# Query and key chunks of the even mixer as k-halves of 512 columns, rotations by token tile

## What is computed

```python
def rotate_pairs(t, cos, sin):
    t1 = t[..., 0::2]
    t2 = t[..., 1::2]
    return jnp.stack([t1 * cos - t2 * sin, t1 * sin + t2 * cos], axis=-1).reshape(t.shape)

def even_mixer(h, w_in, ...):
    q, k, v, g, z, xbc, dt_raw = split_last(h @ w_in, EVEN_SPLITS)   # q, k: 4 heads of 128
    o_ret = retention(q, k, v)          # rotates q and k, then chunked retention
    xbc = silu(causal_conv(xbc) + conv_b)                           # 4 taps, 768 channels
    y = ssd_scan(...)                                                # Mamba-2 heads
    return concat([silu(g) * o_ret, norm(y * silu(z))]) @ w_out
```

## Time and profile before

| | |
|---|---|
| median of three executions | 1211.13 us (1211.05 to 1212.64) |
| profiled execution, its own time | 1211.11 us |
| span of the profiled execution | 1209.2 us |
| TensorE busy | 1197.7 us, 99% |
| VectorE, ScalarE, GpSimd busy | 66%, 53%, 9% |

### The profile page before, as it was taken

How to read it: one execution, slowest core, us unless ns; L and a number is a source line. 1 busy time by engine, 2 the same in 40 slices (tenths; PEclk the granted TensorE clock), 3 DMA queues, 4 the chain that set the end, 5 groups by cost and what they waited for, 6 DMA issues and landing times.

```text
span 1209.2 us, 17908 instructions
## 1 busy us (share of the span) xinstructions
PE 1197.7 (99%) x7109; PEld 1050.6 (87%) x7109; DVE 797.9 (66%) x857; ACT 643.8 (53%) x873; POOL 111.5 (9%) x112
## 2 busy tenths in 40 slices
PE   9999999999999999999999999999999999999997
PEld 8888889989988888888888888899878898888886
DVE  6766766765758576666676666667785686666664
ACT  7555556553457554454564545464666565544443
POOL 1010001640113020000020000020000221100001
PEclk9999999999999999999999999999999999999999
DMA  9966654454444365565555555554642433755550
GB/s 318 346 193 199 183 198 150 147 186 146 139 150 175 105 211 200 181 199 183 174 179 204 192 189 187 195 174 151 198 140 70 141 138 123 243 178 204 176 205 35
DMA packets 166929, 214.76 MB, mean 178 GB/s; under 512 B 14816, under 2 KB 144992, under 8 KB 166752
## 3 DMA queue, kind: packets, MB, share of 16 engines
q1 hardware_dynamic: 166592, 213.29, 53.4%
q0 software_dynamic: 144, 0.52, 0.1%
q10 hardware_dynamic: 144, 0.26, 0.1%
HBM read 213.02 MB, written 1.05 MB: 177 GB/s over the span
## 4 chain that ended last, share of the span: by engine, by line
PE 96%; DVE 2%; ACT 1%; issue 0%; DMA 0%; POOL 0%; POOLq 0%; DVEq 0%; ACTq 0%
PE ps L1987 28%; PE ps L1966 15%; PE ps L1967 15%; PE ps L1968 15%; PE ps L1994 15%; PE ps L2051 1%; PE ps L2639 1%; DVE w_lo L1230 1%; PE ps L2661 1%; PE ps L2506 0%; PE ps L2603 0%; PE ps L2600 0%; DMA arena<-in_first 0%; PE ps L2114 0%; PE ps L2362 0%
## 5 line engine op out<-in xcount | busy, mean ns | idle before, releaser
L1987 PE MATMUL ps<-hT,w_hi 128*128 128x512 f32 x1568 | 374.9, 391 | 1.5 <-ACT w_hi L744 1.4
L1987 PEld LDWEIGHTS ps<-hT,w_hi 128*128 128x128 f32 x1568 | 290.1, 188 | 59.5 <-DVE hT L1270 1.6
L1385 DVE TENSOR_TENSOR w_lo<-raw,w_hi 128x2048 fp32r<-128x2048 f32 x108 | 247.6, 2293 | 61.5 <-ACT w_hi L825 61.5
L1230 DVE TENSOR_TENSOR w_lo<-raw,w_hi 128x2048 fp32r<-128x2048 f32 x85 | 195.6, 2308 | 73.4 <-ACT w_hi L695 73.2
L695 ACT ACTIVATE w_hi<-raw 128x2048 fp32r<-128x2048 f32 x85 | 162.2, 1914 | 92.3 <-PE ps L1968 90.6
L1994 PEld LDWEIGHTS ps<-hT,w_lo 128*128 128x128 f32 x1568 | 201.6, 191 | 8.0
L825 ACT ACTIVATE w_hi<-raw 128x2048 fp32r<-128x2048 f32 x108 | 205.9, 1907 | 0.5 <-DMA raw<-in_ffn_w_gate 0.5
L1994 PE MATMUL ps<-hT,w_lo 128*128 128x256 f32 x1568 | 204.0, 283 | 0.0
L1966 PE MATMUL ps<-w_hi,arena_r 128*128 128x512 f32 x354 | 138.5, 391 | 0.0
L1967 PE MATMUL ps<-w_lo,arena_r 128*128 128x512 f32 x354 | 137.9, 390 | 0.0
L1968 PE MATMUL ps<-w_hi,arena_r 128*128 128x512 f32 x354 | 137.5, 388 | 0.0
(11 more groups left out here) (316 smaller groups left out, 1649.7 us busy)
## 6 DMA issues: line engine op xcount, KB each, us to landing
raw<-in_ffn_w_down SPq DMA_DIRECT2D x44, 1024.0 KB, 4.7
raw<-in_ffn_w_gate SPq DMA_DIRECT2D x43, 1024.0 KB, 5.2
raw<-in_ffn_w_up SPq DMA_DIRECT2D x43, 1024.0 KB, 5.2
raw<-in_xattn_wkv SPq DMA_DIRECT2D x16, 1024.0 KB, 5.4
raw<-in_even_w_in SPq DMA_DIRECT2D x13, 1024.0 KB, 5.0
raw<-in_xattn_wq SPq DMA_DIRECT2D x8, 1024.0 KB, 5.1
raw<-in_xattn_wo SPq DMA_DIRECT2D x8, 1024.0 KB, 4.8
raw<-in_odd_w_in SPq DMA_DIRECT2D x6, 1024.0 KB, 5.5
```

Source lines behind the costliest of these rows:

```text
L1230: ins = V.tensor_tensor(lo, src, hi.bitcast(F32), ALU.subtract)
L1385: V.tensor_tensor(w_lo[:, m % RING, :], raw[:, m % RING, :], w_hi[:, m % RING, :].bitcast(F32), ALU.subtract).then_inc(lo_done, 1)
L1987: mm(ps[:, bank0 + m, :], cols(w_hi, n, k, CW, m * P, (m + 1) * P), hT[:, k, :, :].rearrange("p a c -> p (a c)"), start=k == 0, stop=False)
```

## The change

Chunks 3 to 6 become k-halves of 512 columns, multiplied by `project_half`. The queries of token tile 0 go into bank 0, those of tile 1 into bank 1, the keys of tile 0 into bank 2, those of tile 1 into bank 0 again. A rotation takes one bank, that is, one token tile with its four heads, in four instructions of 256 numbers where there were eight of 128. Rotations 0 and 1 wait for chunks 3 and 4, rotations 2 and 3 for chunks 5 and 6. GpSimd does two operations a rotation where there were four. The low part of chunk 6 is made ahead of rotation 0, where it was made behind it, and each later one is a rotation earlier in the list too. On TensorE, the second tile of chunk 5 waits for `rot_read` 1, since it reuses bank 0.

```diff
@@ pieces_of
-                if s[0] in "vgz":
+                if s[0] != "x":
                     return [(("k", 2 * CW), rows_half(d["even_w_in"][0][:, col:col + 2 * CW], int(s[1])))]
@@ Even
-            rot = [part(5504 + 256 * i, [TT, 2, 64]) for i in range(4)]
+            rot = [part(5504 + 256 * i, [RET_H, 64]) for i in range(4)]
+        ROT_BANK = (0, 1, 2, 0)
@@ VectorE
-            def rotate(e, i):
-                E = at["even", "x0"]
-                dve.wait_ge(chunks_used, E + e + 1)
+            def rotate(i):
+                E, t = at["even", "x0"], i % 2
+                dve.wait_ge(chunks_used, E + (5 if i < 2 else 7))
                 if i:
                     dve.wait_ge(es["rot_done"], i)
-                pair = ps[:, e % 3, :].rearrange("p (t h i two) -> p t h i two", t=TT, h=2, two=2)
...
+                pair = ps[:, ROT_BANK[i], :].rearrange("p (h i two) -> p h i two", h=RET_H, two=2)
+                c, s = (v[:, t, :].unsqueeze(1).to_broadcast([P, RET_H, 64])
+                        for v in (const("cos", TT, 64), const("sin", TT, 64)))
+                for r, (which, table) in enumerate(((0, c), (1, s), (0, s), (1, c))):
+                    ins = V.scalar_tensor_tensor(ev.rot[r], pair[:, :, :, which], rstd[:, t:t + 1], table,
+                                                 ALU.mult, ALU.mult)
                 ins.then_inc(es["rot_read"], 1)
...
                 taps(2)
+                lo_upto(E + 7)
...
-                    rotate(3 + i, i)
-                    lo_upto(E + 3 + i + 4)
+                    rotate(i)
+                    lo_upto(E + 3 + i + 4 + (i < 3))
@@ GpSimd
-                    for t in range(TT):
-                        hs = slice(2 * (i % 2), 2 * (i % 2) + 2)
-                        r = [v[:, t, :, :] for v in (a, b, c, e)]
-                        G.tensor_tensor(dst[:, t, hs, 0, :], r[0], r[1], ALU.subtract)
-                        ins = G.tensor_tensor(dst[:, t, hs, 1, :], r[2], r[3], ALU.add)
+                    G.tensor_tensor(dst[:, i % 2, :, 0, :], a, b, ALU.subtract)
+                    ins = G.tensor_tensor(dst[:, i % 2, :, 1, :], c, e, ALU.add)
@@ TensorE
-                project(3, ("act_read", 1))
-                project(4, ("act_read", 2))
-                project(5, ("act_read", 3))
-                project(6, ("rot_read", 1))
+                project_half(3, 0, (0, 1), (("act_read", 1), ("act_read", 2)))
+                project_half(4, 1, (0, 1))
+                project_half(5, 0, (2, 0), (("act_read", 3), ("rot_read", 1)))
+                project_half(6, 1, (2, 0))
```

More of the change, by code:

```diff
@@ L1504, in cross @@
                 add_residual(wo + 3, 1.0, ("norm", layer, 3))
-            def rotate(e, i):
-                E = at["even", "x0"]
-                dve.wait_ge(chunks_used, E + e + 1)
+            def rotate(i):
+                E, t = at["even", "x0"], i % 2
+                dve.wait_ge(chunks_used, E + (5 if i < 2 else 7))
                 if i:
                     dve.wait_ge(es["rot_done"], i)
-                pair = ps[:, e % 3, :].rearrange("p (t h i two) -> p t h i two", t=TT, h=2, two=2)
-                cosr, sinr = const("cos", TT, 64), const("sin", TT, 64)
-                for t in range(TT):
[L1515 to L1518, removed]
+                pair = ps[:, ROT_BANK[i], :].rearrange("p (h i two) -> p h i two", h=RET_H, two=2)
[4 more added lines that the diff above has]
+                                                 ALU.mult, ALU.mult)
                 ins.then_inc(es["rot_read"], 1)
```

## The result

The changed kernel took 1213.84 us in the median of 20 executions (1212.09 to 1215.56), the kernel before 1211.22 us beside it (1211.02 to 1212.78, 20 executions). The ratio of their means is 1.0015, with a 95% interval of 1.0009 to 1.0021: slower, by about 0.15%. The 20 times lie in three groups, and without them the numbers can't be read: 8 from 1212.1 to 1212.4, 9 from 1213.75 to 1214.2, 3 near 1215.5. The kernel before has two groups: 14 from 1211.0 to 1211.5 and 6 from 1212.6 to 1212.8. The profiled execution of the changed kernel took 1213.89 us, so it is one of the middle group.

What follows compares the result with a forecast made beforehand. TensorE, busy 99% of the span, was taken as the bound: -1.28 us for matmuls, +2.22 for a stall, +0.11 for the restart make +1.05 on 1211.11, so 1212.2 us; range 1209.7 to 1213.4.

Steps and rivals of the forecast that it cites:

- The matmuls: In chunks 3 to 6, 96 matmuls of 512 columns instead of 192 of 256 give back 1.28 us.
- The stall: Before chunk 5's second tile, TensorE waits for rotation 0 to free bank 0, from 231.85 to 234.07: 2.22 us.
- its two causes: On VectorE chunk 6's low part stands ahead of rotation 0; its high part, behind ScalarE's silu, is ready only about 230.2.
- The restart: The first matmul behind TensorE's new wait in chunk 5 adds 0.11 us, with bounds 0 and 0.2.
- The covers: Later rotations, low parts and loads cost nothing; rotation 1 has 5 us to spare, rotation 2 the least, 2.6 us.
- The third rival: Behind the stall in chunk 5 TensorE's clock falls to 1.2 GHz, adding 2.7 us: 1214.9 us; 7 in 100.

Runs made afterwards that it cites:

- the first experiment: The changed kernel with the low part of chunk 6 made behind rotation 0 again: lowest 1209.80 us, median 1210.02, ratio 0.9986 to the kernel before.
- the narrow one: The changed kernel with that low part behind rotation 0 and 192 matmuls of 256 columns, new rotations kept: lowest 1211.00 us, ratio 0.9998 to the kernel before.

## Why the prediction was right, and where it was not

- **The matmuls.** 1.28 us worked out, 1.26 measured by the first experiment and taken back by the narrow one. Right, and the rows decided it: by the issue gaps that the prediction took from the Trainium skill, "TensorE: Matmul & The Clock Gate", section "Back-to-back issue gap", 0.25 would have been left. The page gives those for an isolated matmul and not for a stream.
- **The stall.** TensorE's arrival at 231.85 was 231.89 (231.66 + 0.227), rotation 0 at 232.43 was 232.45, its length of 1.64 us, which no row had shown, was 1.65, the stand of 2.22 was 2.27 from that arrival to the first matmul behind it, at 234.16; the profile counts 2.11, from the end of the last matmul's row (231.66 + 0.39). Undoing either of its two causes takes it away, halving the first halves it, doubling it doubles it. Right.
- **The restart.** 0.11 worked out; 0.34 - 0.23 = 0.11 where the clock held.
- **The covers.** Rotation 1 came at 237.69 and not 237.4, rotation 2 was over at 245.94, 2.7 us ahead of chunk 7's second tile; no other wait came.
- **The third rival.** Here the prediction was wrong in size. It gave a fall of the clock 7 in 100, because TensorE's longest wait before, 1.4 us, had been followed by a granted clock of 1.00. Its "no run shown here has such a fall" holds for its rows, but not for the trace they come from: the last matmul of the kernel before ends at 1202.96, and the granted clock is 1.00 up to 1205.5 and 0.50 from 1205.7 on. That is a fall some 2.6 us behind the last matmul, and the forecast stall of 2.2 us is nearer to it than to 1.4. In the profiled executions the fall came in three of five. Its price was 1.6 us and not 2.7, since eight matmuls ran at the lower level and not twelve; the price in the prediction was an assumption and too high. The forecast and the rival were not two cases with one outcome each, but two outcomes of one kernel, from execution to execution.
- **The numbers.** The forecast of 1212.2 us is the lower group of the executions, 8 of 20. The median of all 20, 1213.84, lies 0.4 us above the range's upper end of 1213.4; the median before times the ratio, 1211.13 x 1.0015 = 1212.9, lies within it. That it does is partly luck: the means, 1211.62 and 1213.50, are 1.9 us apart and not 1.05, and what takes up the rest is the range's stretch for the spread of the kernel before, not a term for the fall. The failing step is the chance of the clock's fall: with one half for it, the range would have had to reach to 1212.2 + 1.6 and the late start's 1.5 on top, 1215.3. The most likely outcome, within 0.2%, was the outcome by the ratio.

## What to carry to other kernels

Where one engine is busy all the time, count the distance between its instructions, not their lengths, and then walk through every new wait on it by the lists of the engines that release it: a step that is moved ahead of the releasing instruction brings the whole wait of that step with it. Here a reordering of two lines cost 2.3 us or more in each profiled execution and turned a gain of 1.3 us into a loss, and putting it back gives the gain. A stall of TensorE can cost more than its length, so a forecast with a new stall should carry the clock's fall as a part of its range, not as a remote case.

## What the hardware showed that was not expected

- Behind a stall of TensorE of 2.1 us its clock went from 2.4 to 1.2 GHz in three of four profiled executions with that stall, for eight matmuls of 512 columns; a stall of 2.8 us did not in one, and one of 4.3 us did, but only after three matmuls at the full rate. Without a stall in the stage no profiled execution had a fall there. The Trainium skill, "TensorE: Matmul & The Clock Gate", section "The HAM clock gate", says that an idle engine has the lower clock, and that the moment of the release at the start varies from run to run. The traces agree with both: the falls above, and the first four matmuls, which took 1.17 us in one profiled execution of the changed kernel and 2.05 in another.
- The table by stretch gives a granted clock of 1.00 for the first microseconds also where the matmuls' distances are doubled (2.04 us for four, not 1.17). The earlier trace rows rested on such a stretch, so it was weaker than it looked: what the clock does there has to be read from the distances. In the kernel before they bear it out, since the first four matmuls take 1.16 us.
- One of GpSimd's two operations of a rotation took 2 us more in some cases and not in others: in rotation 0 the first (2.70 us against 0.72), in rotation 1 neither, in rotation 2 the second (2.78 against 0.74). So it is not always the first behind a wait; what decides it stays open.

```profile
234.19 2.70 POOL L1911 TENSOR_TENSOR arena<-arena 128x256 f32<-128x256 f32 x1 [0.60 <-DVE arena L1518]
236.85 0.72 POOL L1912 TENSOR_TENSOR arena<-arena 128x256 f32<-128x256 f32 x1
239.42 0.74 POOL L1911 TENSOR_TENSOR arena<-arena 128x256 f32<-128x256 f32 x1 [1.85 <-DVE arena L1518]
246.02 0.74 POOL L1911 TENSOR_TENSOR arena<-arena 128x256 f32<-128x256 f32 x1 [5.16 <-DVE arena L1518]
246.72 2.78 POOL L1912 TENSOR_TENSOR arena<-arena 128x256 f32<-128x256 f32 x1
```
